# A mixture-of-experts kernel whose first pass over each expert takes 96 slots in place of 128

## What is computed

```python
def expert_block(args):
    xb, e = args
    h = xb @ w_gate_up[e] + b_gate_up[e]            # [rows, 1024] @ [1024, 2048]
    gate = jnp.minimum(h[:, ::2], SWIGLU_LIMIT)
    up = jnp.clip(h[:, 1::2], -SWIGLU_LIMIT, SWIGLU_LIMIT)
    act = (up + 1.0) * (gate * jax.nn.sigmoid(SWIGLU_ALPHA * gate))
    return act @ w_down[e] + b_down[e]              # [rows, 1024] @ [1024, 1024]
```

## Time and profile before

| | |
|---|---|
| median of 3 runs | 1846.12 us (1846.11 to 1848.58) |
| span of the profiled execution | 1844.5 us |
| TensorE busy in the span | 1792.4 us (97%) |
| VectorE, ScalarE busy | 76%, 60% |
| mixer and router | about 689 us |
| experts | about 1155 us |
| granted TensorE clock, mean | 0.989 of 2.4 GHz |

### The profile page before, as it was taken

One profiled execution on the slowest core, in us unless ns is written; L12 is line 12 of the kernel. 1 busy time (PEld: TensorE's weight loads), 2 busy tenths in 40 slices (PEclk: granted clock), 3 DMA queues, 4 the chain that ended last, 5 costly groups with the idle time before them and its releaser, 6 DMA issues.

```text
span 1844.5 us, 24907 instructions
## 1 busy us (share of the span) xinstructions
PE 1792.4 (97%) x9042; PEld 1478.4 (80%) x9043; DVE 1393.2 (76%) x1263; ACT 1112.7 (60%) x995; POOL 134.1 (7%) x116
## 2 busy tenths in 40 slices
PE   6998999999999979999999999999999999999997
PEld 5886788898888867888888888888888888888885
DVE  3246344427313568999999999999999999999997
ACT  3353322228421345777777777777777777777774
POOL 0000000000000016000000000000000000000001
PEclk9999999999999988999999999999999999999998
DMA  6221132221333468999999999999999999999993
GB/s 215 91 69 69 68 128 91 91 69 37 115 114 137 157 245 281 390 363 369 382 372 368 376 380 363 375 380 368 372 380 373 370 378 375 375 380 372 373 372 128
DMA packets 100599, 493.92 MB, mean 268 GB/s; under 512 B 15562, under 2 KB 17610, under 8 KB 51008
## 3 DMA queue, kind: packets, MB, share of 16 engines
q1 hardware_dynamic: 90640, 475.97, 67.4%
q0 software_dynamic: 9616, 16.62, 3.6%
q10 hardware_dynamic: 288, 0.59, 0.1%
HBM read 484.39 MB, written 25.21 MB: 276 GB/s over the span
## 4 chain that ended last, share of the span: by engine, by line
PE 61%; DVE 1%; ACT 0%; issue 0%; POOL 0%; DVEq 0%; ACTq 0%
PE psum L1813 26%; PE psum L1826 13%; PE psum L1816 13%; PE psum L1831 6%; PE psum L1775 2%; PE psum L1783 2%; PE psum L1806 1%; DVE expert_chunk L1964 0%; DVE h_sb L2130 0%; DVE expert_lo L1661 0%; ACT expert_hi L1656 0%; PE psum L1953 0%; POOL total_rstd L2049 0%; PE psum L1947 0%; ACT up_values L2080 0%
## 5 line engine op out<-in xcount | busy, mean ns | idle before, releaser
L1661 DVE TENSOR_TENSOR expert_lo<-expert_chunk,expert_hi 128x2048 fp32r<-128x2048 f32 x384 | 861.5, 2283 | 45.1 <-ACT expert_hi L1656 43.9
L1656 ACT CAST expert_hi<-expert_chunk 128x2048 fp32r<-128x2048 f32 x384 | 735.6, 1918 | 225.9 <-PE psum L1816 193.8
L265 DVE TENSOR_TENSOR chunk_lo<-chunk,chunk_hi 128x2048 fp32r<-128x2048 f32 x48 | 109.9, 2289 | 272.9 <-ACT chunk_hi L261 272.8
L1813 PE MATMUL psum<-expert_hi,rowsT_hi 128*128 128x512 f32 x992 | 272.9, 397 | 0.0
L1813 PE MATMUL psum<-expert_hi,rowsT_lo 128*128 128x512 f32 x992 | 266.5, 390 | 0.0
L1816 PE MATMUL psum<-expert_lo,rowsT_hi 128*128 128x512 f32 x992 | 266.0, 390 | 0.0
L1813 PEld LDWEIGHTS psum<-expert_hi,rowsT_lo 128*128 128x128 f32 x992 | 186.8, 188 | 39.9
L1816 PEld LDWEIGHTS psum<-expert_lo,rowsT_hi 128*128 128x128 f32 x992 | 186.8, 188 | 39.0
L1813 PEld LDWEIGHTS psum<-expert_hi,rowsT_hi 128*128 128x128 f32 x992 | 182.3, 189 | 42.2 <-issue 7.8
L261 ACT CAST chunk_hi<-chunk 128x2048 fp32r<-128x2048 f32 x48 | 91.7, 1911 | 195.5 <-PE psum L296 167.3
L296 PE MATMUL psum<-chunk_hi,xT_hi 128*128 128x512 f32 x480 | 189.3, 394 | 5.3 <-DVE chunk_lo L265 3.6
(11 more groups left out here) (292 smaller groups left out, 1912.5 us busy)
## 6 DMA issues: line engine op xcount, KB each, us to landing
expert_chunk<-in_expert_w_gate_up SPq DMA_DIRECT2D x256, 1024.0 KB, 7.6
expert_chunk<-in_expert_w_down SPq DMA_DIRECT2D x128, 1024.0 KB, 7.0
chunk<-in_w_in SPq DMA_DIRECT2D x38, 1024.0 KB, 4.9
chunk<-in_w_branch_gla SPq DMA_DIRECT2D x4, 1024.0 KB, 5.1
chunk<-in_w_mix_out SPq DMA_DIRECT2D x4, 1024.0 KB, 5.2
gla_v<-in_x SPq DMA_DIRECT2D x4, 512.0 KB, 8.4
y_glaT_away<-h_sb SPq DMA_DIRECT2D x1, 2048.0 KB, 7.7
att_qT_then_y_glaT<-y_glaT_away SPq DMA_DIRECT2D x1, 2048.0 KB, 7.6
```

What stands on the lines that cost most here:

```text
L265: dve.tensor_tensor(self.wlo[c][:], self.raw[c][:], self.whi[c][:].bitcast(F32), ALU.subtract).then_inc(self.lo_done[c], 1)
L1656: act.copy(self.expert_hi[c % self.SLOTS][:], self.expert_ring[c % self.RING][:]).then_inc(self.moe["hi"], 1)
L1661: dve.tensor_tensor(self.expert_lo[s][:], self.expert_ring[c % self.RING][:], self.expert_hi[s][:].bitcast(F32), ALU.subtract).then_inc(se ...
L1813: pe.matmul(bank, x[:, k, :], whi[s][:, m // 2, m % 2 * COLS:(m % 2 + 1) * COLS], start=False, stop=False)
```

## The change

The first pass takes 96 slots. `FIRST_SLOTS = 96` stands in the place of `P` wherever the slots of an expert are meant:

- the stationary tiles of all expert products have 96 columns, their results 96 partitions; the weights that move are the same (512 columns);
- the transposes take 96 partitions of rows as the stationary operand (still 128 columns of them) and move a 96 by 96 identity, so they write 96 columns;
- the splits of the turned rows take 384 elements of each partition in place of 512; element-wise work on slots takes 96 partitions with the same 1024 or 512 elements in each;
- gather and scatter take 96 indices;
- a token ranked beyond 96 goes to a further block. `further_places` compares with 96, 224, 352 and 480 in place of 128, 256 and 384, so it has one comparison and one addition more; the number of possible further blocks rises from 16 to 21, with the two tables `block_starts_sb` and `blocks_before` and the loop of `further_blocks`.

Weights, loads of weights and their splits, the order of the work, the waits and the mixer stay as they are.

```diff
+FIRST_SLOTS = 96
+MOST_FURTHER = SEQ * TOP_K // (FIRST_SLOTS + 1)
...
-        pool.indirect_dma_start(self.h[:, 0, :], None, self.normed, bass.IndirectOffsetOnAxis(ap=self.index[u][:, 0:1], axis=0),
+        pool.indirect_dma_start(self.h[0:FIRST_SLOTS, 0, :], None, self.normed,
+                                bass.IndirectOffsetOnAxis(ap=self.index[u][0:FIRST_SLOTS, 0:1], axis=0),
...
-        link(dve.tensor_scalar(extra[:], counts, float(P), None, ALU.is_gt))
-        for n in range(2, NB):
-            link(dve.tensor_scalar(past[:], counts, float(n * P), None, ALU.is_gt))
+        link(dve.tensor_scalar(extra[:], counts, float(FIRST_SLOTS), None, ALU.is_gt))
+        for n in range(1, NB):
+            link(dve.tensor_scalar(past[:], counts, float(FIRST_SLOTS + n * P), None, ALU.is_gt))
             link(dve.tensor_tensor(extra[:], extra[:], past[:], ALU.add))
...
+        taken = slice(0, FIRST_SLOTS)
...
+        turned = lambda f: self.bank[6 + f][:, 0:HALF_KT * FIRST_SLOTS].rearrange("p (k n) -> p k n", n=FIRST_SLOTS)
...
-                    last = pe.transpose(self.bank[6 + f][:, k * P:(k + 1) * P],
-                                        rows[:, (HALF_KT * f + k) * P:(HALF_KT * f + k + 1) * P], self.ident[:])
+                    last = pe.transpose(turned(f)[:, k, :], rows[taken, (HALF_KT * f + k) * P:(HALF_KT * f + k + 1) * P],
+                                        self.ident[taken, taken])
...
-                act.copy(dst[:, HALF_KT * f:HALF_KT * (f + 1), :],
-                         self.bank[6 + f].rearrange("p (k n) -> p k n", n=P)).then_inc(done, 1)
+                act.copy(dst[:, HALF_KT * f:HALF_KT * (f + 1), :], turned(f)).then_inc(done, 1)
...
-                    pe.matmul(bank, x[:, k, :], whi[s][:, m // 2, m % 2 * COLS:(m % 2 + 1) * COLS], start=False, stop=False)
+                    pe.matmul(bank[taken, :], x[:, k, :], whi[s][:, m // 2, m % 2 * COLS:(m % 2 + 1) * COLS], start=False, stop=False)
...
-            act.activation(sg[:], gv[:], ACT.Sigmoid, scale=SWIGLU_ALPHA).then_inc(S["sig"], 1)
+            act.activation(sg[taken, :], gv[taken, :], ACT.Sigmoid, scale=SWIGLU_ALPHA).then_inc(S["sig"], 1)
...
-                pe.matmul(sums[b][:, m, :], hotT[:, b, :], y_hi[:, m * COLS:(m + 1) * COLS], start=False, stop=False)
+                pe.matmul(sums[b][:, m, :], hotT[taken, b, :], y_hi[:, m * COLS:(m + 1) * COLS], start=False, stop=False)
```

More of the change, by code:

```diff
@@ L1723, in further_places @@
         link(dve.tensor_scalar(past[:], run[:], float(P), None, ALU.mult))
-        link(dve.tensor_scalar(extra[:], extra[:], -float(P), -float(P), ALU.mult, ALU.add))
+        link(dve.tensor_scalar(extra[:], extra[:], -float(P), -float(FIRST_SLOTS), ALU.mult, ALU.add))
         link(dve.tensor_tensor(extra[:], extra[:], past[:], ALU.add))
-        link(dve.tensor_scalar(far[:], self.rank[:], float(P + 1), None, ALU.is_ge))
+        link(dve.tensor_scalar(far[:], self.rank[:], float(FIRST_SLOTS + 1), None, ALU.is_ge))
         link(dve.tensor_tensor(self.place[:], self.rank[:], extra[:].unsqueeze(1).to_broadcast([P, NB, E]), ALU.add))
@@ L1782, in turn_act, with turned_hi @@
                 for k in range(HALF_KT):
-                    last = pe.transpose(self.bank[6 + f][:, k * P:(k + 1) * P],
-                                        a[:, (HALF_KT * f + k) * P:(HALF_KT * f + k + 1) * P], self.ident[:])
+                    last = pe.transpose(turned(f)[:, k, :], a[taken, (HALF_KT * f + k) * P:(HALF_KT * f + k + 1) * P],
+                                        self.ident[taken, taken])
                 last.then_inc(S["act_turned"], 1)
-        def turned_hi(act, e, turned, done, dst):
+        def turned_hi(act, e, in_bank, done, dst):
             for f in range(2):
-                act.wait_ge(turned, 2 * e + f + 1)
-                act.copy(dst[:, HALF_KT * f:HALF_KT * (f + 1), :],
-                         self.bank[6 + f].rearrange("p (k n) -> p k n", n=P)).then_inc(done, 1)
+                act.wait_ge(in_bank, 2 * e + f + 1)
+                act.copy(dst[:, HALF_KT * f:HALF_KT * (f + 1), :], turned(f)).then_inc(done, 1)
         def turned_lo(dve, e, hi_done, done, hi_t, dst):
@@ L1796, in turned_lo @@
                 dve.wait_ge(hi_done, 2 * e + f + 1)
[L1797 to L1798 removed]
+                dve.tensor_tensor(dst[:, at, :], turned(f), hi_t[:, at, :].bitcast(F32), ALU.subtract).then_inc(done, 1)
         def gate_up_bias(pe, e0, i=0):
@@ L1805, in gate_up_bias @@
                 at = slice(m * (P // 4), (m + 1) * (P // 4))
-                pe.matmul(bank, self.ones[at, :], self.bias_rows[e0 % 2][at, :].bitcast(F32R), start=True, stop=False)
+                pe.matmul(bank[taken, :], self.ones[at, taken], self.bias_rows[e0 % 2][at, :].bitcast(F32R), start=True, stop=False)
         def gate_up_chunk(pe, c, i, k, rows_hi=x_hi, rows_lo=x_lo):
@@ L1830, in down_chunk @@
                 for m, bank in enumerate(banks):
-                    last = pe.matmul(bank, acts[0][:, 2 * q + kk, :], wlo[s][:, kk, m * COLS:(m + 1) * COLS], start=False,
+                    last = pe.matmul(bank[taken, :], acts[0][:, 2 * q + kk, :], wlo[s][:, kk, m * COLS:(m + 1) * COLS], start=False,
                                      stop=(q == 3 and kk == 1))
@@ L1900, in swiglu_p @@
             dve.wait_ge(S["gu"], 2 * e + 2)
-            dve.scalar_tensor_tensor(out=uv[:], in0=uv[:], scalar=1.0, in1=gv[:], op0=ALU.add,
+            dve.scalar_tensor_tensor(out=uv[taken, :], in0=uv[taken, :], scalar=1.0, in1=gv[taken, :], op0=ALU.add,
                                      op1=ALU.mult).then_inc(S["p"], 1)
@@ L1957, in lo_products @@
                 pe.wait_ge(S["y_lo"], m + 1)
-                last = pe.matmul(sums[b][:, m, :], hotT[:, b, :], y_lo[:, m * COLS:(m + 1) * COLS], start=False, stop=True)
+                last = pe.matmul(sums[b][:, m, :], hotT[taken, b, :], y_lo[:, m * COLS:(m + 1) * COLS], start=False, stop=True)
             last.then_inc(S["totals"], 1)
@@ L2022, in _ @@
                 self.last_row = pool.to_reg(SEQ - 1)
-                last = pool.to_reg((P + 1) * E - 1)
+                last = pool.to_reg((FIRST_SLOTS + 1) * E - 1)
                 pool.wait_ge(S["table_cleared"], 16)
@@ L2101, in _ @@
                 over_bodies(dve, body_dve)
-                first = self.body_chunk(LAST, 0)
+                tail = self.body_chunk(LAST, 0)
                 turned_lo(dve, LAST, S["aT_hi"], S["aT_lo"], x_hi, x_lo)
-                for c in range(first, first + 4):
+                for c in range(tail, tail + 4):
                     lo(dve, c)
@@ L2110, in _ @@
                     dve.wait_ge(S["y_hi"], m + 1)
-                    dve.scalar_tensor_tensor(out=y_lo[:, at], in0=bank, scalar=weight[LAST % self.UNROLL][:, 0:1],
+                    dve.scalar_tensor_tensor(out=y_lo[:, at], in0=bank[taken, :], scalar=weight[LAST % self.UNROLL][taken, 0:1],
                                              in1=y_hi[:, at].bitcast(F32), op0=ALU.mult,
@@ L2157, in _ @@
                 for q in range(4):
-                    down_chunk(pe, first + q, 0, q, banks=last_banks, acts=self.rowsT)
+                    down_chunk(pe, tail + q, 0, q, banks=last_banks, acts=(x_hi, x_lo))
                 pe.wait_ge(S["hot"], 3)
```

46 lines of the change are left out of this document (24 added, 22 removed).

## The result

| | before | after |
|---|---|---|
| median | 1846.11 us (six runs, 1844.52 to 1848.58) | 1856.53 us (six runs, 1853.72 to 1862.67) |
| profiled span | 1844.5 us | 1860.9 us (run of 1862.67) |
| start of the first body | 688.95 us | 689.33 us |
| first three bodies | 33.45, 38.03, 35.11 us | 32.38, 44.53, 43.42 us |
| a body of the loop, mean | 35.10 us | 35.18 us |

The changed kernel is slower: ratio 1.0061, 95% interval 1.005 to 1.0072, 10.4 us on the medians. 1831.0 us was forecast. (Bodies are measured from one group of bias products to the next.) The profiled run of after was the longest of its six, so its trace holds some 6 us more than the median.

What follows compares the result with a forecast made beforehand. TensorE was taken to bound the expert stage. Transposes -13.6, open loads -1.6 and start +0.1 sum to -15.1 us on the 1844.5 us span: 1829.4, as a median 1831.0 us; range for 8 in 10, 1815 to 1847 us.

Steps and rivals of the forecast that it cites:

- Part 1: The 4608 expert products: 96 stationary columns change nothing, as the load hides under the 512-column moving stream; cost 0.
- fourth rival: Expert products: 96 columns cost more, priced at 6 ns each, 1858.6 us; decides from 3.3 ns a product; chance 0.13.
- The row called nearest: Trace row for stationary width: two groups of four transposes, 96 and 128 columns, both 0.44 us; cited for unchanged products.
- Part 2: The 512 transposes: 32 fewer moving columns cut each step from 109 to 82 ns, -13.6 us.
- Part 3: Loads not hidden, ahead of bias products and the first product after them: 26 ns less each, -1.6 us.
- Part 4: Router's end and first expert: longer `further_places` +0.44 us, shorter first splits -0.25 us, sum +0.1 us.
- Part 5: Splits inside bodies, element-wise work, gather and scatter of 96 indices: none on the chain, so 0.
- Part 6: Further blocks: not run, since the fullest expert has 90 tokens, under 96; 0.
- rivals of transfers: DMA in the expert stage: 373 GB/s is the limit, bodies stay at 35.1 us, 1846 us; chance 0.06.
- load-paced transposes: Transposes: their load sets the step, so their gain is absent, 1844.6 to 1846.2 us; chance 0.09.
- signs of being wrong: A product group changes, TensorE waits for `expert_lo` or a landing, or its clock falls to the 1.2 GHz level.
- product rival: Expert products with 96 columns cost more: 6 ns each, 27.6 us in all, 1858.6 us; chance 0.13.

Runs made afterwards that it cites:

- e6: After with its products 128 stationary columns wide in place of 96: 1846.05 us, ratio 0.9999 to before.
- e15: After with clamps, p, sigmoid and product with the sigmoid on 128 partitions again: 1848.54 us, ratio 1.0016 to before.
- e3: Before with only the transposes and the splits of what they turned at 96 slots: 1833.65 us, ratio 0.9937 to before.
- e2: Before with only gather and scatter taking 96 indices: 1845.45 us, ratio 1.0002 to before.
- e4: Before with only the products (and bias products) at 96 stationary columns: 1857.82 us, ratio 1.0062 to before.
- e8: Before with products of 112 stationary columns: 1865.76 us, one run.
- e11: Before with products of 64 stationary columns, rows of slots 64 to 127 left out: 1854.05 us, one run.
- e16: Before with only VectorE's four element-wise operations on 96 partitions: 1851.76 us, ratio 1.0036 to before.
- e14: Before with transposes and splits at 96 slots, plus VectorE's p and product with the sigmoid on 96 partitions: 1840.09 us, one run.
- e13: Before with transposes and splits at 96 slots, plus only VectorE's two clamps on 96 partitions: 1864.92 us, one run.
- e9: Before with transposes and splits at 96 slots, plus VectorE's four element-wise operations on 96 partitions: 1849.21 us, ratio 1.0015 to before.

## Why the prediction was wrong

**Part 1, products at no cost: wrong, the step that failed first.** The argument was that only the moving stream sets the step, so a shorter load under it changes nothing. The shorter load is there (188 to 162 ns), but the step rose by 3 to 4 ns, and it rose (by 3 to 5 ns) at each of the three widths short of 128 that were run. It was the fourth rival, which had a chance of 0.13 and said that no row excluded it. Its 6 ns were too much; 0.44 us / 144 = 3.0 ns by the bodies (e6 to after) and 4.0 ns by the starts of products lie around its breaking point of 3.3 ns. So by itself it only eats the gain, as e15 shows (+2.8 us). The row called nearest, four transposes that took 0.44 us with 96 and with 128 columns, moved 128 columns and not 512, and at two digits could not show 3 ns. The bounds should have been set on both sides by the scatter of the step after a break, 224 to 236 ns in before; I gave only the settled value 226. Why a full-width product settles into the short step and a narrower one doesn't stays open.

**Part 2, transposes -13.6 us: right.** 82 ns each, 12.4 us by e3's bodies. The load rule of the Trainium skill that spoke against it ("TensorE: Matmul & The Clock Gate", section LDWEIGHTS) does not hold for transposes here: by it 107 ns would have been the floor.

**Part 3, open loads -1.6 us: half of it shown.** The bias group takes 0.40 in place of 0.44 us, 1.2 us in 31 bodies where the forecast had 0.8. The group behind it takes 2.01 us, which before has in every second body too (2.04 and 2.01 by turns), and its products are slower now, so what the load gave there can't be told.

**Part 4, the start +0.1 us: can't be told.** It moved by 0.4 us (688.95 to 689.33), but in before, e2, e4, e8, e11 and e16, which have the same first part, the first body starts anywhere from 687.9 to 691.3 us.

**Part 5, the work beside at 0: wrong, and nearly as dear.** VectorE's own time was right (134.58 to 131.86 us over four bodies). I costed the element-wise operations by their durations, which stayed, and asked only whether TensorE waits for them. I did not ask what they do to GpSimd, whose list placements, gathers and last scatter do stand ahead of TensorE. Before had the sign of it: a placement lasted 0.98 us when VectorE was not splitting and 3.03 us beside a split. Timelines of before, GpSimd and then VectorE:

```profile
721.13 0.98 POOL L1691 DMA_INDIRECT slots_of_experts<-choice_token_and_weight,choice_row_of_table  x1 [0.30 <-issue]
...
725.69 3.03 POOL L1691 DMA_INDIRECT slots_of_experts<-choice_token_and_weight,choice_row_of_table  x1 [0.30 <-issue]
```
```profile
725.58 2.28 DVE L1661 TENSOR_TENSOR expert_lo<-expert_chunk,expert_hi 128x2048 fp32r<-128x2048 f32 x1
```

725.69 + 3.03 = 728.72 us, 0.86 us after the split's end at 727.86. In after the 14.04 us placement ends at 740.16 us, 0.85 us after a split that VectorE starts at 737.03 and ends at 739.31, the last of five in a row while the placement was held:

```profile
728.23 11.09 DVE L1665 TENSOR_TENSOR expert_lo<-expert_chunk,expert_hi 128x2048 fp32r<-128x2048 f32 x5
```

So a held placement or gather ended behind the end of a VectorE operation, by nearly what it takes alone (0.98 us), and the question is at which end. The scatters are less regular. The price of such misses is 5 to 9 us where a gather or a placement is hit, 4 us for the last scatter, and in after nothing for the other scatters: ScalarE waits 3.4 us a body for them (92.9 us in all) beside TensorE's work, and a body is 35.18 us as in e15, where they are short.

**Part 6 and the rivals of transfers and of load-paced transposes**: further blocks did not run, e3 moves its chunks in 34.70 us bodies, and the transposes took 82 ns. Right to give them little.

The forecast's sum lacked 3 ns x 4608 for the products and 8 to 11 us for the holds. Two of the signs of being wrong that it named are in the profile of after: a group of products changed, and TensorE waited for `expert_lo` and for a landing. The range ended at 1847 us, at "no change", with the product rival left out; a mechanism that no row excludes and whose breaking point is 1.5% of a step needed its place in the range.

## What to carry to other kernels

A change that leaves every duration on the busiest engine alone can still move its step by 1 to 2% when a tile stops being full; over 4608 instructions that equals the gain of the change, so try the narrow tile apart from the rest. Narrow only what is paid by the slot (here the moving side of a transpose) and leave the operations whose time does not depend on the partition count (a clamp takes 1.21 us on 96 and on 128) at their full 128. When an edit touches VectorE, look in the profile at how long GpSimd's DMA instructions last beside it, and follow those that something waits for.

## What the runs showed of the hardware

- A weight load of 188, 162 or 134 ns (128, 96, 64 columns) hides under a 512-column product at every width, and the product's step is shortest at 128: 227.1 ns against 231.7 (112), 230.1 (96), 230.0 (64).
- GpSimd's indirect DMA instructions were held while VectorE ran its splits, and held placements and gathers ended 0.79 to 0.94 us after the end of a VectorE operation. In every kernel with VectorE's elem on 128 partitions that was the first split's end, and none lasted over 3.1 us; with 96 partitions some missed several ends (14.04 us for a placement, 9.8 for a gather, and 7 to 8 for scatters). In e3 and e14 a placement starts 0.11 us after the start of a split; in e3 it lasts 3.03 us, in e14, where the operations on either side of the split are on 96 partitions, 8.57 us. Yet e13's held gather had no such operation next to its start, nor had e9's second held placement (6.30 us), which started among splits alone. Why 96 partitions bring the missed ends was not found; no kernel tried another partition count.
- The Trainium skill, "SBUF — State Buffer", section "Who interferes with whom", has VectorE's and GpSimd's shared ports as an exclusive lock. It says that a `tensor_tensor` with both inputs in SBUF, as the splits are, contends with GpSimd's reads, and infers that it does not stall the writing of DMA descriptors. Here the placement beside a split takes 3.03 in place of 0.98 us. That fits the first statement if the instruction counts as one that reads SBUF, and speaks against the inference otherwise; no run here tells the two apart.
- After a wait of 5.0 us TensorE lost another 3.2 us in its next groups: the granted clock was 0.50, the 1.2 GHz level, from 800.32 to 806.70 us, and 1.00 from 810.20 to 1800 us.
